# Six more chunks by seven block products in the last MLP group, their side products added at the end of each unit

## Chip, core and metric

One core of one Trainium2 chip. The metric is the device time of one execution in microseconds. The kernel before took 2679.48 us in the median of three runs (2678.41 to 2681.5).

## What is computed

Two layers of a streaming encoder on 256 rows of 2048 columns in fp32, and a final RMSNorm. The part that matters here is the MLP at the end of a layer:

```python
for l in range(DEPTH):                      # DEPTH = 2
    ...
    h = rmsnorm(x, norm_mlp[l])
    x = x + jnp.square(jax.nn.relu(h @ w_up[l])) @ w_down[l]    # 2048 -> 8192 -> 2048
return rmsnorm(x, final_norm)
```

## The kernel before

**Chunks.** All weights run through one stream of chunks. A chunk holds 256 rows of K by 512 output columns (128 partitions x 1024 fp32, 512 KB). A unit is eight chunks, K = 2048 into one block of 512 output columns. The two row tiles t of 128 rows fill two PSUM banks `acc[bank][t]`.

**Splits.** fp32 precision comes from three matmuls of rounded values: hi x hi, hi x lo, lo x hi. For each chunk SP loads `raw[c % 4]`, ACT copies it to `w_hi[c % 4]` (L865), DVE subtracts to get `w_lo[c % 4]` (L1281), and PE multiplies. There are four buffers of each. ACT waits until PE has finished chunk c-4 (`multiplied`), and SP waits for `lo_ready` of chunk c-4 before it loads chunk c. Each engine runs its own program in order, written out by hand in `unit` of ACT and of DVE: `at` puts a job ahead of a chunk's split, `then` behind it.

**Two kinds of chunk.** A plain chunk is 12 matmuls of 512 columns (L522 to L524, in the interleaved units L538 to L540, in the last unit L552 to L554). A chunk by seven products, `seven_products` at L476, sees the chunk's 256 x 512 weights and the 256 x 256 activations as 2 x 2 blocks and needs 7 block products in place of 8, a Strassen-Winograd form: 21 matmuls of 256 columns (L490 to L492). For it DVE forms sums of weight blocks (`weight_sums`, L1290 to L1296) and the split is 1792 columns wide (ACT L872 and L874, DVE L1302). Sums of activation blocks must be there too: for the hidden activations u they are made in `u_moved` (L1767 to L1772), copied by ACT (`u_sums_hi`, L1197) and split by DVE (`u_sums_lo`, L1776). Four of the seven products are accumulated in two side banks, `wide_acc`. `take_sides` (L1782) reads these into `rest` in SBUF, and `add_sides` (L1787 to L1791) combines the four quarters of a block and adds them to x.

**The MLP.** K and columns of the hidden layer are taken in four groups of 2048. The first three run in a loop `Fori` with many seven-product chunks. The last group is written out after the loop: up unit 2 (chunks 1, 3, 5, 7 by seven products), up unit 3 (plain), then four down units for the four blocks of x. Down units 0 and 1 are interleaved (PE L836 to L850) since the blocks of u arrive one by one. Then come down unit 2, and down unit 3, in the second layer as `last_unit`, which takes row tile 0 of its chunks 4 to 7 first and row tile 1 of these behind.

**Blocks of u.** After an up unit ACT applies relu and square into `stage`, DVE transposes in 32x32 pieces (`spread_u`, L1359), a DMA writes to scratch in HBM and four DMAs read it back into `moved`, ACT and DVE split that into `o_hl` (L932, L1383). Blocks 1 and 2 are passed on by POOL, block 3 by SP, in `load_down(GROUPS - 1, 0, pass_on(l, E_LAST), late=True, ...)`: SP issues all loads of down unit 0, then waits for the spread, stores, waits, fetches, and only then loads the first chunk of unit 1.

**The end of a down unit** n: DVE adds the banks to block n of x (`add_to_x`, L1700, two instructions of 128x512), ACT then squares that block for the norm (`square_block`, L949), and in the second layer DVE multiplies with the final gain (`gain_block`, L1798). These jobs lie in the chunk stream of the next unit. The four side sums of the loop, in `rest`, are added to x by `add_sides(0)` in up unit 3, `(1)` in the interleaved stretch, `(2)` and `(3)` later, wherever DVE's list has them. In the last group the DVE lines of before are:

```python
run(C_MLP + 64 * g + 32, (), {3: second_and_third, 5: lambda: add_sides(1)})
for n in range(1, NBLK):
    def x_add(n=n):
        add_to_x(base + 64 * g + (42 if n == 1 else 32 + 8 * n), n - 1)
    ...
    then = {3 if n > 1 else 5: x_add}
    ...
    if n < NBLK - 1:
        then[3 if n == 1 else 5] = lambda n=n: add_sides(n + 1)
```

`42` is the unit-0 end: the tenth chunk of the interleaved sixteen is the last of unit 0.

Of the kernel before, what the change touches and what calls it, by code (L numbers as in the profile page):

```python
# [5 lines left out]
ALU = mybir.AluOpType  # L6
ACT = mybir.ActivationFunctionType
# [8 lines left out]
DEPTH = 2  # L16
# [75 lines left out]
U_SUMS = (GROUPS - 1) * NBLK  # L92
SHARED = ((0, 1, 2, 3, 4, 5, 8, 9), (-2, -1, 2, 3, 4, 5, 6, 7))
# [17 lines left out]
def trunk_kernel(nc, x, w_misc, w_main, gains, sinks, rel_bias, onehot, final_gain, bias_rows, out):  # L111
    with ExitStack() as ctx:
# [354 lines left out]
        def _(pe):  # L467
# [248 lines left out]
            for l in range(DEPTH):  # L716
# [130 lines left out]
                for c in range(8, 10):
                    plain(two, c, c - 2, o_lhs, acc[0])
                for c in range(10, 16):
                    plain(two, c, c - 8, o_lhs, acc[1])  # L850
                down(last + 48, 0, adds(GROUPS - 1, 1), 2)
# [7 lines left out]
        def _(act):  # L859
# [186 lines left out]
            for l in range(DEPTH):  # L1046
# [168 lines left out]
                with act.Fori(0, GROUPS - 1) as g:  # L1215
# [25 lines left out]
                run(C_MLP + 64 * g + 32, (), {3: second_and_third})  # L1241
                for n in range(1, NBLK):
                    def x_take(n=n):
                        act.wait_ge(dve_took, l * DVE_UNITS + (12 + 4 * (GROUPS - 1) + n + 1))
                        square_block(n - 1, l * (2 * NBLK) + (2 * NBLK + n - 1))
# [10 lines left out]
                    run(C_MLP + 64 * g + 32 + 8 * n, (), then)  # L1256
# [17 lines left out]
        def _(dve):  # L1274
# [313 lines left out]
            for l in range(DEPTH):  # L1588
# [168 lines left out]
                def u_moved(g, n, sums=True):  # L1757
# [6 lines left out]
                    steps = g * (3 * NBLK) + (l * U_SUMS * 3 + 3 * n)  # L1764
                    a11, a21, a12, a22 = (moved_pieces()[:, a] for a in range(4, 8))
# [59 lines left out]
                with dve.Fori(0, GROUPS - 1) as g:  # L1825
# [26 lines left out]
                run(C_MLP + 64 * g + 16, (), {2: lambda: u_moved(g, 0, False), 3: lambda: spread_u(g, 1)},  # L1852
                    WIDE_UP[2], steps_at(g, AT_UP2))
                run(C_MLP + 64 * g + 24, {3: lambda: add_up_sides(g, 2, NBLK)},
                    {2: lambda: u_moved(g, 1, False), 4: lambda: spread_u(g, 2), 6: lambda: add_sides(0)})

                def second_and_third():
                    u_moved(g, 2, False)
                    spread_u(g, 3)
                run(C_MLP + 64 * g + 32, (), {3: second_and_third, 5: lambda: add_sides(1)})  # L1860
                for n in range(1, NBLK):
                    def x_add(n=n):
                        add_to_x(base + 64 * g + (42 if n == 1 else 32 + 8 * n), n - 1)
                        if l < DEPTH - 1:
                            spread_x(E_XD + n - 1, n - 1, 12 + 4 * g + n)
# [6 lines left out]
                    if n < NBLK - 1:  # L1872
                        then[3 if n == 1 else 5] = lambda n=n: add_sides(n + 1)
# [6 lines left out]
                    run(C_MLP + 64 * g + 32 + 8 * n, (), then)  # L1880
# [103 lines left out]
```

## Time and profile before

| | us |
|---|---|
| median of three runs | 2679.48 |
| profiled execution | 2679.57 |
| its span, first to last instruction | 2677.8 |
| PE busy | 2662.2 (99%) |
| PE weight load busy | 2231.3 (83%) |
| DVE busy | 2048.7 (77%) |
| ACT busy | 1446.9 (54%) |
| POOL busy | 128.4 (5%) |

Busy time is the time in which an engine's instructions run; PE's weight loads overlap its matmuls. The chain that ended last is 92% PE. A plain share of the span says nothing on a single stretch: for that the rows below are from timelines (start, duration, and in brackets how long the engine idled before an instruction and what ended it) and from windows.

### The profile page before, as it was taken

What the parts mean: (1) busy time and instruction counts of PE and PEld (TensorE: products, weight loads), DVE (VectorE), ACT (ScalarE), POOL (GpSimd) and SP (SyncE); (2) the same over time, 40 slices, a digit from 0 to 9 for tenths busy, and PEclk for the clock granted to TensorE, in tenths of its full rate; (3) what the DMA queues carried; (4) which work ended last, traced back from release to release, by engine and by line L of the source; (5) the groups of instructions that cost most, each with busy time, mean ns of one, the idle gap of its engine ahead of it and who ended that gap; (6) DMA issues with size and microseconds to landing.
All of it is one profiled execution on the core that took longest, in us unless ns stands there. A gap on an engine that the chain in (4) does not pass through costs nothing.

```text
span 2677.8 us, 37183 instructions
## 1 busy us (share of the span) xinstructions
PE 2662.2 (99%) x13544; PEld 2231.3 (83%) x13544; DVE 2048.7 (77%) x3016; ACT 1446.9 (54%) x1861; POOL 128.4 (5%) x220
## 2 busy tenths in 40 slices
PE   9999999999999999999999999999999999999998
PEld 7788778888888888888887887788888888888886
DVE  5665568977798897987756655689678988989875
ACT  5545555555665555645445455555456556556554
POOL 0100000000100100100010000000001000000000
PEclk9999999999999999999999999999999999999999
DMA  7874545676775766766687655466677667667574
GB/s 258 240 232 166 181 158 183 224 245 233 233 233 190 242 220 203 243 208 232 228 238 224 214 173 177 156 202 224 227 258 235 226 202 237 213 219 231 190 248 150
DMA packets 179959, 575.53 MB, mean 215 GB/s; under 512 B 23016, under 2 KB 43028, under 8 KB 179664
## 3 DMA queue, kind: packets, MB, share of 16 engines
q1 hardware_dynamic: 166400, 537.21, 60.8%
q0 software_dynamic: 13008, 35.98, 5.2%
q8 instruction: 106, 1.74, 0.3%
q14 instruction: 61, 0.50, 0.1%
q10 hardware_dynamic: 384, 0.11, 0.0%
HBM read 535.15 MB, written 38.04 MB: 214 GB/s over the span
## 4 chain that ended last, share of the span: by engine, by line
PE 92%; DVE 4%; DMA 2%; issue 1%; ACT 1%; DVEq 0%; POOLq 0%; ACTq 0%; POOL 0%; SPq 0%
PE acc L522 24%; PE acc L524 23%; PE acc L523 23%; PE att L490 2%; PE att L492 2%; PE att L491 2%; PE acc L490 2%; PE acc L492 2%; PE acc L491 2%; DMA raw<-in_w_main 1%; DVE w_lo L1281 1%; PE acc L539 1%; PE acc L538 1%; PE acc L540 1%; DVE w_lo L1302 1%
## 5 line engine op out<-in xcount | busy, mean ns | idle before, releaser
L1281 DVE TENSOR_TENSOR w_lo<-raw,w_hi 128x1024 fp32r<-128x1024 f32 (+1 forms) x778 | 935.3, 1213 | 422.7 <-ACT w_hi L865 419.9
L865 ACT ACTIVATE w_hi<-raw 128x1024 fp32r<-128x1024 f32 (+1 forms) x778 | 813.7, 1051 | 676.9 <-PE acc L524 499.1
L522 PE MATMUL acc<-w_hi,h_hl 128*128 128x512 f32 x1848 | 736.6, 399 | 1.0 <-DVE w_lo L1281 1.0
L524 PE MATMUL acc<-w_hi,h_hl 128*128 128x512 f32 x1848 | 729.0, 394 | 0.0
L523 PE MATMUL acc<-w_lo,h_hl 128*128 128x512 f32 x1848 | 728.5, 394 | 0.0
L522 PEld LDWEIGHTS acc<-w_hi,h_hl 128*128 128x128 f32 x1848 | 347.9, 188 | 83.7 <-issue 5.5
L524 PEld LDWEIGHTS acc<-w_hi,h_hl 128*128 128x128 f32 x1848 | 347.9, 188 | 81.4
L523 PEld LDWEIGHTS acc<-w_lo,h_hl 128*128 128x128 f32 x1848 | 348.3, 188 | 75.9
L1302 DVE TENSOR_TENSOR w_lo<-raw,w_hi 128x1792 fp32r<-128x1792 f32 x166 | 335.6, 2022 | 40.5 <-ACT w_hi L874 39.4
L522 PE MATMUL acc<-w_hi,o_hl 128*128 128x512 f32 x912 | 360.9, 396 | 0.0
L523 PE MATMUL acc<-w_lo,o_hl 128*128 128x512 f32 x912 | 359.9, 395 | 0.0
L524 PE MATMUL acc<-w_hi,o_hl 128*128 128x512 f32 x912 | 359.7, 394 | 0.0
L872 ACT ACTIVATE w_hi<-raw 128x768 fp32r<-128x768 f32 x166 | 140.3, 845 | 197.5 <-PE acc L492 112.9
L874 ACT ACTIVATE w_hi<-raw 128x1024 fp32r<-128x1024 f32 x166 | 174.8, 1053 | 82.3 <-DVE raw L1296 82.2
L524 PEld LDWEIGHTS acc<-w_hi,o_hl 128*128 128x128 f32 x912 | 171.7, 188 | 40.3
L522 PEld LDWEIGHTS acc<-w_hi,o_hl 128*128 128x128 f32 x912 | 171.6, 188 | 37.4 <-issue 1.4
L523 PEld LDWEIGHTS acc<-w_lo,o_hl 128*128 128x128 f32 x912 | 171.7, 188 | 36.0
L1290 DVE TENSOR_TENSOR raw<-raw 128x512 f32<-128x512 f32 x166 | 113.4, 683 | 15.1 <-DMA raw<-in_w_main 8.9
L1359 DVE STREAM_TRANSPOSE spread<-stage 128x512 f32<-128x512 f32 x112 | 73.0, 689 | 22.9 <-ACT stage L1068 19.8
L963 ACT ACTIVATE probs<-probs,low 128x128 f32<-128x128 f32 x96 | 41.0, 428 | 69.1 <-DVE sink_d L1510 44.0
L1294 DVE TENSOR_TENSOR raw<-raw 128x256 f32<-128x256 f32 x166 | 70.6, 425 | 5.8
L1296 DVE TENSOR_TENSOR raw<-raw 128x256 f32<-128x256 f32 x166 | 70.6, 425 | 5.7
(279 smaller groups left out, 3474.7 us busy)
## 6 DMA issues: line engine op xcount, KB each, us to landing
raw<-in_w_main SPq DMA_DIRECT2D x928, 512.0 KB, 4.2
scratch<-spread SPq DMA_DIRECT2D x37, 512.0 KB, 2.8
moved<-scratch SPq DMA_DIRECT2D x148, 128.0 KB, 3.3
scratch<-spread POOLq DMA_DIRECT2D x30, 512.0 KB, 3.5
moved<-scratch POOLq DMA_DIRECT2D x120, 128.0 KB, 4.9
raw<-in_w_misc SPq DMA_DIRECT2D x16, 336.0 KB, 3.8
bias_b<-bias_rows POOLq DMA_DIRECT2D x32, 96.0 KB, 5.3
xs<-in_x SPq DMA_DIRECT2D x4, 512.0 KB, 7.2
```

Source lines behind the costliest of these rows:

```text
L490: nc.tensor.matmul(o, a_hi, hi[:, w], start=start, stop=False, skip_group_check=True)
L491: nc.tensor.matmul(o, a_hi, lo[:, w], start=False, stop=False, skip_group_check=True)
L492: return nc.tensor.matmul(o, a_lo, hi[:, w], start=False, stop=stop, skip_group_check=True)
L522: nc.tensor.matmul(o, a_hi, hi[:, kk], start=(k == 0), stop=False)
L523: nc.tensor.matmul(o, a_hi, lo[:, kk], start=False, stop=False)
L524: last = nc.tensor.matmul(o, a_lo, hi[:, kk], start=False, stop=fin)
L865: nc.scalar.activation(w_hi[s][:, 0:2 * width], raw[r][:, 0:2 * width], ACT.Copy).then_inc(hi_ready, 1)
L872: nc.scalar.activation(w_hi[s][:, 0:3 * HALF], raw[s][:, HALF:CW], ACT.Copy)
L874: nc.scalar.activation(w_hi[s][:, 3 * HALF:7 * HALF], raw[s][:, CW:2 * CW], ACT.Copy).then_inc(hi_ready, 1)
L1281: nc.vector.tensor_tensor(w_lo[s][:, 0:2 * width], raw[r][:, 0:2 * width], w_hi[s][:, 0:2 * width].bitcast(F32), ALU.subtract).then_inc(lo ...
L1290: nc.vector.tensor_tensor(r[:, 4 * HALF:6 * HALF].rearrange("p (k n) -> p k n", k=2), r[:, HALF:3 * HALF].rearrange("p (k n) -> p k n", k= ...
L1302: nc.vector.tensor_tensor(w_lo[s][:, 0:7 * HALF], raw[s][:, HALF:8 * HALF], w_hi[s][:, 0:7 * HALF].bitcast(F32), ALU.subtract).then_inc(lo ...
```

## The change

In the second layer's last group, two of the eight chunks of K of each of down units 0, 1 and 2 are multiplied by seven block products: `END_WIDE = ((1, 3), (3, 5), (1, 3))`. In the order of loads, with the 32 down chunks numbered 0 to 31, these are 1, 3, 11, 13, 17 and 19. With it come: the sums of u for blocks 0, 1 and 2 of the last group, on DVE and ACT; weight sums and wide splits for the six chunks; a read of the side banks (`take_sides`) and the combination (`add_sides`) for blocks 0, 1 and 2 once their unit is done, just ahead of `add_to_x`. The earlier `add_sides(0)`, `(1)`, `(2)` are gone in this layer; `add_sides(3)` stays. ACT's squares of both layers' last groups write to `stage` and no longer to `att[2]`, now a side bank.

```diff
+END_WIDE = ((1, 3), (3, 5), (1, 3))
 ...
+                def chunk(at, c, n):
+                    if c in ends[n]:
+                        pe.wait_ge(sums_took, u_sums_took(GROUPS - 1, c // 2))
+                        pe.wait_ge(lo_ready, two + (RAW + at + 1))
+                        seven_products(c, acc[n], o_lhs, u_sum, wide_acc[1 - n], ends[n]).then_inc(multiplied, 1)
+                    else:
+                        plain(two, at, c, o_lhs, acc[n])
 ...
-                down(last + 48, 0, adds(GROUPS - 1, 1), 2)
+                down(last + 48, 0, adds(GROUPS - 1, 1), 2, wide=ends[2])
 ...
-                run(C_MLP + 64 * g + 32, (), {3: second_and_third})
+                run(C_MLP + 64 * g + 32, (), {3: second_and_third, 4: end_sums(2)}, ends[0], steps_at(g, END_AT[0]))
 ...
-                        square_block(n - 1, l * (2 * NBLK) + (2 * NBLK + n - 1))
+                        square_block(n - 1, l * (2 * NBLK) + (2 * NBLK + n - 1), stage)
 ...
+                    if isinstance(g, int) and n:
+                        dve.wait_ge(sums_took, g * NBLK + (l * U_SUMS + n))
 ...
+                def first_and_spread():
+                    if final:
+                        u_sums_lo(g, 1)
+                    spread_u(g, 2)
 ...
-                    {2: lambda: u_moved(g, 1, False), 4: lambda: spread_u(g, 2), 6: lambda: add_sides(0)})
+                    {2: lambda: u_moved(g, 1, final), 4: first_and_spread, 6: (lambda: None) if final else (lambda: add_sides(0))})
 ...
                     def x_add(n=n):
-                        add_to_x(base + 64 * g + (42 if n == 1 else 32 + 8 * n), n - 1)
+                        at = base + 64 * g + (42 if n == 1 else 32 + 8 * n)
+                        if final:
+                            unit_done(at)
+                            chain.link(take_sides(n - 1))
+                            add_sides(n - 1)
+                        add_to_x(at, n - 1)
 ...
-                    if n < NBLK - 1:
+                    if n == 2 or (n == 1 and not final):
                         then[3 if n == 1 else 5] = lambda n=n: add_sides(n + 1)
 ...
-                    run(C_MLP + 64 * g + 32 + 8 * n, (), then)
+                    run(C_MLP + 64 * g + 32 + 8 * n, (), then, ends[n] if n < 3 else (), steps_at(g, END_AT[n]) if n < 3 else None)
```

On DVE, the splits of down chunks 12 to 16 of the second layer, with block 0 of x between those of 13 and 14. Before:

```order
L1281 TENSOR_TENSOR w_lo0<-raw0,w_hi0 128x1024 [waits hi_ready,dve_chain]
L1281 TENSOR_TENSOR w_lo1<-raw1,w_hi1 128x1024 [waits hi_ready]
L1700 TENSOR_TENSOR xs<-acc00,xs 128x512 [waits multiplied]
L1700 TENSOR_TENSOR xs<-acc01,xs 128x512
L1281 TENSOR_TENSOR w_lo2<-raw2,w_hi2 128x1024 [waits hi_ready]
L1798 TENSOR_TENSOR xs<-xs,bias_a 128x512 [waits final_loaded,sq_done]
L1798 TENSOR_TENSOR xs<-xs,bias_a 128x512
L1281 TENSOR_TENSOR w_lo3<-raw3,w_hi3 128x1024 [waits hi_ready]
```

Now (the first row is the split of chunk 12, `w_lo1` is chunk 13, `w_lo2` is 14):

```order
L1298 TENSOR_TENSOR w_lo0<-raw0,w_hi0 128x1024 [waits hi_ready]
L1319 TENSOR_TENSOR w_lo1<-raw1,w_hi1 128x1792 [waits hi_ready]
L1801 TENSOR_TENSOR qk<-att2,qk 128x512 [waits multiplied]
L1801 TENSOR_TENSOR qk<-turn,qk 128x512
L1807 TENSOR_TENSOR qk<-qk 128x256 [waits dve_chain]
L1808 TENSOR_TENSOR qk<-qk 128x256 [waits dve_chain]
L1809 TENSOR_TENSOR qk<-qk 128x256
L1810 TENSOR_TENSOR qk<-qk 128x256 [waits dve_chain]
L1811 TENSOR_TENSOR xs<-xs,qk 128x2x512 [waits dve_chain]
L1717 TENSOR_TENSOR xs<-acc00,xs 128x512 [waits multiplied,dve_chain]
L1717 TENSOR_TENSOR xs<-acc01,xs 128x512
L1298 TENSOR_TENSOR w_lo2<-raw2,w_hi2 128x1024 [waits hi_ready]
```

The read of `att2` and `turn` and the five instructions of the combination stand between the split of chunk 13 and the addition to x; the split of chunk 14 moved behind them. Around block 1 (chunks 19, 20) and block 2 (chunks 27, 28) the same is found.

On DVE, up unit 3 from the split of its chunk 2 to that of its chunk 3. Before:

```order
L1281 TENSOR_TENSOR w_lo2<-raw2,w_hi2 128x1024 [waits hi_ready]
L1383 TENSOR_TENSOR o_hl<-moved,o_hl 128x1024 [waits moved_hi]
L1671 TENSOR_TENSOR stage2<-att2,stage 128x256 [waits sides_out]
L1673 TENSOR_TENSOR stage<-stage2,turn 128x2x256 [waits up_step]
L1676 TENSOR_TENSOR stage<-stage,turn 128x256 [waits up_step]
L1677 TENSOR_TENSOR stage<-acc00,stage 128x512
L1679 TENSOR_TENSOR stage<-acc01,stage 128x512 [waits up_step]
L1281 TENSOR_TENSOR w_lo3<-raw3,w_hi3 128x1024 [waits hi_ready]
```

Now:

```order
L1298 TENSOR_TENSOR w_lo2<-raw2,w_hi2 128x1024 [waits hi_ready]
L1400 TENSOR_TENSOR o_hl<-moved,o_hl 128x1024 [waits moved_hi]
L1786 TENSOR_TENSOR stage2<-moved 128x128 [waits sums_took]
L1787 TENSOR_TENSOR stage2<-moved 128x128
L1789 TENSOR_TENSOR stage2<-stage2,moved 128x128 [waits sum_step]
L1791 TENSOR_TENSOR stage2<-moved,stage2 128x128 [waits sum_step]
L1688 TENSOR_TENSOR stage2<-att2,stage 128x256 [waits sides_out]
L1690 TENSOR_TENSOR stage<-stage2,turn 128x2x256 [waits up_step]
L1693 TENSOR_TENSOR stage<-stage,turn 128x256 [waits up_step]
L1694 TENSOR_TENSOR stage<-acc00,stage 128x512
L1696 TENSOR_TENSOR stage<-acc01,stage 128x512 [waits up_step]
L1298 TENSOR_TENSOR w_lo3<-raw3,w_hi3 128x1024 [waits hi_ready]
```

Four sums of u block 1 stand ahead of the side additions of up unit 2 (L1671 to L1679 before, L1688 to L1696 now).

## Rows read from the trace of the kernel before

**Rows 1.** Windows: length, busy of PE, PEld, DVE, ACT, POOL; clock, DMA, GB/s.
```profile
2568.20:2646.30 78.10, 78.10 (x337) 63.30 (x337) 55.86 (x64) 36.24 (x42) 2.77 (x5) 1.00 0.70 227
```

**Rows 2.** Timeline of PE: start us, us, engine, line, operation, tiles, shape.
```profile
2453.07 0.28 PE L490 MATMUL att<-w_hi,m_hl 128*128 128x256 f32 x1
...
2455.56 0.39 PE L522 MATMUL acc<-w_hi,o_hl 128*128 128x512 f32 x1
...
2646.32 0.40 PE L552 MATMUL acc<-w_hi,o_hl 128*128 128x512 f32 x1
...
2668.41 0.40 PE L554 MATMUL acc<-w_hi,o_hl 128*128 128x512 f32 x1
```

**Rows 3.** Timeline of ACT and DVE, last unit; [idle before <-what ended it].
```profile
2646.58 1.06 ACT L865 ACTIVATE w_hi<-raw 128x1024 fp32r<-128x1024 f32 x1 [1.72 <-PE acc L524]
...
2647.68 1.23 DVE L1281 TENSOR_TENSOR w_lo<-raw,w_hi 128x1024 fp32r<-128x1024 f32 x1 [1.55 <-ACT w_hi L865]
2648.82 1.28 DVE L1700 TENSOR_TENSOR xs<-acc,xs 128x512 f32<-128x512 f32 x2
...
2650.13 0.60 ACT L949 ACTIVATE att<-xs 128x512 f32<-128x512 f32 x1 [2.49 <-DVE xs L1700]
...
2651.52 1.99 ACT L865 ACTIVATE w_hi<-raw 128x1024 fp32r<-128x1024 f32 x2
...
2652.59 2.36 DVE L1281 TENSOR_TENSOR w_lo<-raw,w_hi 128x1024 fp32r<-128x1024 f32 x2 [2.50 <-ACT w_hi L865]
```

**Rows 4.** Timeline of DVE: u sums in loop; up units 2 and 3.
```profile
2418.84 0.28 DVE L1767 TENSOR_TENSOR stage<-moved 128x128 f32<-128x128 f32 x1
...
2419.94 1.31 DVE L1359 STREAM_TRANSPOSE spread<-stage 128x512 f32<-128x512 f32 x2
...
2540.30 2.02 DVE L1302 TENSOR_TENSOR w_lo<-raw,w_hi 128x1792 fp32r<-128x1792 f32 x1 [1.95 <-ACT w_hi L874]
...
2566.71 1.23 DVE L1281 TENSOR_TENSOR w_lo<-raw,w_hi 128x1024 fp32r<-128x1024 f32 x1 [2.31 <-ACT w_hi L865]
```

**Rows 5.** Timeline of DVE, loop end: side read, wide split, weight sums.
```profile
2521.73 1.28 DVE L1782 TENSOR_TENSOR qk<-att,qk 128x512 f32<-128x512 f32 x2
...
2532.53 2.03 DVE L1302 TENSOR_TENSOR w_lo<-raw,w_hi 128x1792 fp32r<-128x1792 f32 x1 [2.30 <-ACT w_hi L874]
2534.48 0.69 DVE L1290 TENSOR_TENSOR raw<-raw 128x512 f32<-128x512 f32 x1
...
2536.00 1.22 DVE L1281 TENSOR_TENSOR w_lo<-raw,w_hi 128x1024 fp32r<-128x1024 f32 x1
```

**Rows 6.** Timeline of SP, the hand-over of u block 3.
```profile
2586.49 0.33 SPq L324 DMA_DIRECT2D scratch<-spread  x1
...
2590.88 0.91 SPq L308 DMA_DIRECT2D raw<-in_w_main  x2
```

**Rows 7.** Timeline of ACT: the split of down chunk 8.
```profile
2595.77 1.06 ACT L865 ACTIVATE w_hi<-raw 128x1024 fp32r<-128x1024 f32 x1 [3.90 <-DMA raw<-in_w_main]
```

**Rows 8.** Timeline of DVE: addition of side products, next split.
```profile
2604.20 0.42 DVE L1787 TENSOR_TENSOR qk<-qk 128x256 f32<-128x256 f32 x1
...
2607.17 1.22 DVE L1281 TENSOR_TENSOR w_lo<-raw,w_hi 128x1024 fp32r<-128x1024 f32 x1
```

**Rows 9.** Timeline of ACT: the two copies of a seven-product chunk.
```profile
2538.49 0.82 ACT L872 ACTIVATE w_hi<-raw 128x768 fp32r<-128x768 f32 x1
2539.22 1.04 ACT L874 ACTIVATE w_hi<-raw 128x1024 fp32r<-128x1024 f32 x1
```

**Rows 10.** Timeline of DVE, last unit: gain, reduction, last split.
```profile
2657.19 1.29 DVE L1798 TENSOR_TENSOR xs<-xs,bias_a 128x512 f32<-128x512 f32 x2
2658.39 0.15 DVE L1801 TENSOR_REDUCE mean_sq<-squares 128x2 f32<-128x6 f32 x1
...
2658.90 1.23 DVE L1281 TENSOR_TENSOR w_lo<-raw,w_hi 128x1024 fp32r<-128x1024 f32 x1
```

**Rows 11.** Windows, after the last matmul; columns as in Rows 1.
```profile
2674.00:2675.00 1.00, 0.00 (x0) 0.00 (x0) 0.00 (x0) 0.00 (x0) 0.00 (x0) 0.50 1.10 352
```

More of the change, by code:

```diff
@@ L835, in _ @@
                 two = l * CHUNKS + last + 32
+                ends = END_WIDE if l == DEPTH - 1 else ((), (), ())
+                def chunk(at, c, n):
[5 more added lines that the diff above has]
+                        plain(two, at, c, o_lhs, acc[n])
                 acts(GROUPS - 1, 3)()
@@ L943, in hi_moved_x, with square_block @@
                 last.then_inc(moved_hi, 1)
-            def square_block(n, before):
+            def square_block(n, before, over=None):
                 for t in range(TT):
                     act.wait_ge(sq_done, before * TT + t)
-                    nc.scalar.activation(att[2][:], xs[:, t, n * NB:(n + 1) * NB], ACT.Square,
+                    nc.scalar.activation(att[2][:] if over is None else over[:, t, :], xs[:, t, n * NB:(n + 1) * NB], ACT.Square,
                                                 accum_out=squares[:, t, n:n + 1]).then_inc(sq_done, 1)
@@ L1232, in _, with end_sums @@
                 g, end = GROUPS - 1, base + 64 * (GROUPS - 1)
-                run(C_MLP + 64 * g + 16, {3: lambda: take_up(g, 1, end + 16, 1)}, {2: lambda: u_moved(g, 0)},
+                ends = END_WIDE if l == DEPTH - 1 else ((), (), ())
+                def end_sums(n):
+                    return (lambda: u_sums_hi(g, n)) if l == DEPTH - 1 else (lambda: None)
+                run(C_MLP + 64 * g + 16, {3: lambda: take_up(g, 1, end + 16, 1)}, {2: lambda: u_moved(g, 0), 6: end_sums(0)},
                     WIDE_UP[2], steps_at(g, AT_UP2))
                 run(C_MLP + 64 * g + 24, {3: lambda: take_side(g, 2, end + 24), 4: lambda: take_summed(g, 2, sides_count(g, 0))},
-                    {2: lambda: u_moved(g, 1)})
+                    {2: lambda: u_moved(g, 1), 3: end_sums(1)})
                 def second_and_third():
@@ L1879, in _ @@
                         then[6] = lambda n=n: gain_block(n - 1)
-                    run(C_MLP + 64 * g + 32 + 8 * n, (), then)
+                    run(C_MLP + 64 * g + 32 + 8 * n, (), then, ends[n] if n < 3 else (), steps_at(g, END_AT[n]) if n < 3 else None)
                 if l < DEPTH - 1:
```

30 lines of the change are left out of this document (21 added, 9 removed).

## The prediction

> **What bounds the kernel now.** I read the busy time by stretch first. From 2568.20 to 2646.30 us, most of the last group, PE is busy for the whole stretch at a granted clock of 1.00 [rows 1]. It waits for nothing there, so the stage costs what its matmuls cost, and every chunk that PE takes faster is a gain as long as its split is ready in time. The second view is PE's timeline, for the price of a chunk. The chunk by seven products in the loop starts at 2453.07 and the next plain one at 2455.56, which is 2.49 us. The last unit runs from 2646.32 to the last matmul at 2668.41 plus one step of 0.23, 22.32 us for eight plain chunks, or 2.79 us each [rows 2]. The third view is the timeline of ACT and DVE, because they feed PE: a chunk is split by ACT, then by DVE, and ACT may start on chunk c only when PE has finished chunk c-4. So the lead is four chunks of PE time: 4 x 2.79 = 11.16 us for plain ones. In the last unit PE finishes the unit before at 2646.32, ACT starts at 2646.58, DVE at 2647.68, the addition to x at 2648.82, the squares at 2650.13, ACT's next split at 2651.52, DVE's at 2652.59 [rows 3]. That DVE split ends 1.23 later, 7.50 us after the release, so 3.7 us of the lead are left. This slack is what the change spends.
>
> I number the 32 down chunks of the group 0 to 31 as SP loads them (0 to 15 are units 0 and 1 interleaved, 16 to 23 unit 2, 24 to 31 unit 3). Seven products: 1, 3, 11, 13, 17, 19. Counting back at 2.79, PE starts chunk 0 at 2579.36 and chunk 8 at 2601.68 in the run before.
>
> **Part 1, the seven products.** Six chunks at 2.49 in place of 2.79 are 6 x 0.30 = 1.8 us less on PE, all on the path. That is the whole gain.
>
> **Part 2, sums of u and of weights.** Each of three u blocks now gets its four small sums on DVE: 1.10 us from the first of them to the next instruction in the loop (2418.84 to 2419.94) [rows 4]. A split of the sums (128x512, estimated at 0.6, half of the 1.14 for twice the width) and an ACT copy follow. Block 0's lie in up unit 2, where DVE idles 1.95 us ahead of its split of 2540.30: nothing. Block 1's stand directly ahead of the side additions and of the splits of up unit 3's chunks 3 and 4. DVE's split of chunk 4 starts at 2566.71 there and ends at 2567.94 [rows 4]; PE wants it at 2579.36 - 4 x 2.79 = 2568.20. The slack is 0.26, the addition 1.10, so PE waits 0.84; the split of the sums stands behind it, and I take **1.0**, with 0 and 1.4 as ends.
> Each seven-product chunk costs DVE the weight sums, 2534.48 to 2536.00, 1.52 us, and a split of 1.95 (2532.53 to 2534.48) in place of 1.14 [rows 5]: 2.33 more, for a chunk that PE finishes 0.3 sooner. Chunks 1 and 3 stand before block 3 is spread. SP sends that spread on before it loads chunk 8: the store is issued at 2586.49, chunk 8's load only at 2590.88 [rows 6], and ACT gets it at 2595.77 after waiting 3.90 us for the DMA [rows 7]. Ahead of the spread DVE gets two sets of sums (2.2), a split of sums (0.6) and 2 x 2.33, and loses one side addition (2.97): 4.5 us more, some of it into idle time, so the load comes 0 to 4.5 later. Block 3 is ready about 3.5 us after ACT's start, at 2599.2, and PE wants it at 2601.68, or at 2602.1 with the 1.0 and 2 x 0.3 above. Stall 0 to 1.7; I take **0.5**.
>
> **Part 3, the side products, added when a unit is done.** Before, the additions (2604.20 to 2607.17, 2.97 us) [rows 8] ran in idle time of DVE. Now they stand between the end of a unit and the addition to x, behind a read of the side banks: two instructions of 128x512 from PSUM, 1.28 us as in the loop [rows 5]. ACT stands waiting for that addition with its squares, and behind the squares is its next split. That is a wait of two engines in a chain, 4.25 us longer than before.
> Unit 2, block 2 (chunk 28, all plain), from the release: 0.26 + 1.10 + 1.14 (ACT and DVE split of chunk 27), + 1.28 + 2.97 + 1.31 (addition to x, till the squares start) + 1.39 (squares) + 1.07 + 1.23 = 11.75 us, against a lead of 11.16 [rows 3, 5, 8]. Late by 0.6.
> Blocks 0 and 1 (chunks 14 and 20) have a seven-product chunk as the last one split, so ACT takes 0.73 + 1.06 and DVE 1.95 in place of 1.10 and 1.14 [rows 5, 9], and two of the four chunks of the lead are short ones. The chain is 13.3 us against 2 x 2.79 + 2 x 2.49 = 10.56: late by 2.7 each, even if DVE arrives with nothing queued.
> DVE does arrive with work queued. Counted from the start of its split of chunk 14: PE reaches chunk 20 at 1.23 + 4 x 2.79 + 2 x 2.49 = 17.4. DVE has chunk 14 (1.14), the gain (1.20), 15, sums of 17 (1.52), 16, 17 (1.95), sums of 19, 18 and 19: 12.7 us. Then 1.28 + 2.97 + 1.31 + 1.39 + 1.07 + 1.23 = 9.25, together 21.95. Chunk 20 is late by **4.6**. For chunk 14 I take **3.3**, between 2.7 and the 4.6 of chunk 20, nearer the low end since chunks 4 to 10 are plain. For chunk 28, splits and loads of 20 to 27 come late too (a load is issued only when DVE has split the chunk four before): 0.6 to 1.5, I take **1.0**.
> Chunk 31: PE's last unit takes only row tile 0 of chunks 28 to 31 first, so it wants them every 1.40 us. DVE has 29 and 30, the gain (1.20), a reduction with its follow-up (2658.39 to 2658.90, 0.51) and then chunk 31 [rows 10]. From chunk 28's DVE start: 3 x 1.14 + 1.20 + 0.51 + 1.23 = 6.36, and PE wants it at 1.23 + 4.19 = 5.42. Late by **0.9**.
> The squares go to SBUF and not to a PSUM bank. The nearest row, a copy to SBUF, takes 1.06 us for 1024 columns, the square to PSUM 0.60 for 512 [rows 3], so 0.1 us either way for each of the two, and I take 0. In the first layer nothing else changes. The tail behind the last matmul is the same.
>
> **Sum.** -1.8 + 1.0 + 0.5 + 3.3 + 4.6 + 1.0 + 0.9 = +9.5 us. The profiled execution took 2679.57 us (span 2677.8), 0.09 above the median of the three timed runs. 2679.57 + 9.5 = **2689.1 us**, 0.36% slower.
>
> **Rivals.**
> A, the forecast: the longer chain outruns the lead and DVE's queue adds to it.
> B, only the bare chains: DVE has caught up at each of the three places and the early stalls are hidden. 2 x 2.7 + 0.6 + 0.9 - 1.8 = +5.1, 2684.7 us. For it: DVE does catch up before, as its idle 1.95 us ahead of 2540.30 shows [rows 4]. Against it: the 12.7 us of listed work between chunks 14 and 20 leave no idle time.
> C, the lead covers the additions and PE never waits: 2679.57 - 1.8 = 2677.8 us, faster than before by less than 0.2%. It decides at the chain's length: read and additions (4.25 us) would have to take under 1.5 us together, or ACT would have to split ahead of the squares, which its order does not do. For it speaks only that PE never waits there now. A partial cover ends within 0.2% of before.
> D, PE's clock falls. At the end of the program PE starts its last matmul at 2668.41 [rows 2], and the clock is 0.50, the lower level of 1.2 GHz, in the stretch from 2674 to 2675 [rows 11]: at most 5.6 us of idleness brought it. The stall ahead of chunk 20 (4.6) comes near that. At half clock one chunk costs 2.79 more; with one such chunk the time is 2691.9 us.
> The Trainium skill ("TensorE: Matmul & The Clock Gate", Part 1) says that an idle array falls back to 1.2 GHz by itself and needs sustained activity to return. By that rule D could set in at shorter stalls than the tail shows, at the price just given; the trace agrees with it as to the level only.
>
> **How the numbers follow.** A 0.64, B 0.14, D 0.14, C with partial cover 0.08. The upper end takes the high ends of the terms (1.4, 1.7, 4.6, 5.4 for chunk 20 with a late load, 1.5, 0.9): 15.5 - 1.8 = +13.7, 2693.3, and a clock drop on a middling case reaches 2695. The lower end is B's, 2684.5. Below it lies C. About 0.2% (5.4 us, so 2684.8) is what a measurement of this kernel can tell from no change: B falls on that line, and I count about two in five of it as the same, with C. More than 0.2% of gain is out of reach, since PE can save 1.8 us only. Slower 0.85, same 0.14, faster 0.01.
>
> **What would show it.** In the profile after, PE should have idle time at four places in the last 90 us, each put down to DVE's w_lo: 2.7 to 4.6 us ahead of chunk 14, 3 to 5 ahead of chunk 20, 0.6 to 1.5 ahead of 28, about 0.9 in the first pass over 31; and under 1.5 in up unit 3. The six chunks should take 2.49. ACT's wait for the addition to x, 2.5 us before, should read about 7. If PE waits nowhere, C is right and the reading of the lead is wrong. If the stalls are as said but the time is higher, look for a granted clock under 1.00.

## The result and the profile after

The changed kernel takes 2692.64 us in the median of six runs (2689.64 to 2695.77), the kernel before 2681.15 in the median of six beside them (2678.41 to 2683.51). The ratio is 1.0045, with a 95% interval of 1.0034 to 1.0055: slower by 11.5 us, where the forecast had 9.5. Against the forecast time of 2689.1 it is 3.5 us above; 1.7 of that is the kernel before, which came out slower in these six runs than in the three that the forecast started from. The profiled execution took 2691.67 us.

The measure for the rest is a stretch of PE's timeline, from the first matmul of up unit 2's sums (`s_hh`) to the last matmul of the program. Before it is 129.59 us (2538.82 to 2668.41, the end is in [rows 2]), after 140.77 us (2539.80 to 2680.57): +11.18. Of the 12.1 us between the two profiled executions the rest, 1.0, is there before the stretch starts; the tail behind the last matmul is the same within 0.1. Runs of one kernel differ by up to 6 us end to end, so the experiments below are compared by this stretch. How far the stretch itself varies between runs of one kernel was not measured; differences of a few tenths are read only where a single gap shows them.

The window over most of the last group, which answers to [rows 1]: length, busy of PE, PEld, DVE, ACT, POOL, then clock, DMA share, GB/s.

```profile
2568.00:2646.00 78.00, 71.02 (x354) 59.13 (x353) 63.53 (x79) 39.16 (x48) 2.76 (x5) 0.97 0.59 195
```

PE was busy for all of this stretch before; now it is idle for 7 us of it, and the clock is below 1.00. PE's timeline after shows where (in brackets the idle time ahead of an instruction and what ended it):

```profile
2603.05 0.50 PE L540 MATMUL acc<-w_hi,o_hl 128*128 128x512 f32 x1 [0.36 <-DVE o_hl L1400]
...
2619.16 0.28 PE L494 MATMUL acc<-w_hi,o_hl 128*128 128x256 f32 x1
2623.11 0.51 PE L540 MATMUL acc<-w_hi,o_hl 128*128 128x512 f32 x1 [3.67 <-DVE w_lo L1298]
...
2623.96 0.63 PE L540 MATMUL acc<-w_hi,o_hl 128*128 128x512 f32 x1
...
2627.33 0.39 PE L542 MATMUL acc<-w_hi,o_hl 128*128 128x512 f32 x1
2627.56 0.39 PE L540 MATMUL acc<-w_hi,o_hl 128*128 128x512 f32 x1
...
2640.77 0.28 PE L494 MATMUL acc<-w_hi,o_hl 128*128 128x256 f32 x1
2644.00 0.53 PE L524 MATMUL acc<-w_hi,o_hl 128*128 128x512 f32 x1 [2.95 <-DVE w_lo L1298]
```

These are chunks 8, 14 and 20, all at the places forecast. Behind the two long stalls a matmul of 512 columns starts 0.43 us after the one before it, and 0.23 once that is over. The waits of the last 160 us (engine, its tile and line, what it waited for, us in total, times, longest) add chunks 28 and 31 (L554) and ACT's wait for the addition to x:

```profile
ACT stage L961 <- DVE xs L1717: 22.0, 3, 7.6
...
PE acc L540 <- DVE w_lo L1298: 3.7, 1, 3.7
...
PE acc L524 <- DVE w_lo L1298: 3.0, 1, 3.0
...
PE acc L554 <- DVE w_lo L1298: 1.0, 2, 0.5
```

**The chain ahead of chunk 14**, DVE's timeline after. It answers to the last-unit rows of [rows 3]: there the addition to x followed a split directly; now the read (L1801) and the combination (L1807 to L1811) stand between them.

```profile
2611.82 2.03 DVE L1319 TENSOR_TENSOR w_lo<-raw,w_hi 128x1792 fp32r<-128x1792 f32 x1
2613.77 0.68 DVE L1801 TENSOR_TENSOR qk<-att,qk 128x512 f32<-128x512 f32 x1
2614.37 0.68 DVE L1801 TENSOR_TENSOR qk<-turn,qk 128x512 f32<-128x512 f32 x1
2615.08 0.42 DVE L1807 TENSOR_TENSOR qk<-qk 128x256 f32<-128x256 f32 x1
...
2616.79 1.22 DVE L1811 TENSOR_TENSOR xs<-xs,qk 128x1024 f32<-128x1024 f32 x1
2618.05 1.29 DVE L1717 TENSOR_TENSOR xs<-acc,xs 128x512 f32<-128x512 f32 x2
2621.83 1.23 DVE L1298 TENSOR_TENSOR w_lo<-raw,w_hi 128x1024 fp32r<-128x1024 f32 x1 [2.49 <-ACT w_hi L877]
```

And ACT's timeline in the same microseconds:

```profile
2610.73 1.06 ACT L886 ACTIVATE w_hi<-raw 128x1024 fp32r<-128x1024 f32 x1 [0.80 <-DVE raw L1313]
2619.37 0.63 ACT L961 ACTIVATE stage<-xs 128x512 f32<-128x512 f32 x1 [7.58 <-DVE xs L1717]
...
2620.76 2.93 ACT L877 ACTIVATE w_hi<-raw 128x1024 fp32r<-128x1024 f32 x3
```

Read them together: ACT has nothing to do from 2611.79 to 2619.37, because the squares are next in its order and they want the addition. The split of chunk 14 is behind the squares, so DVE waits for ACT in turn (2.49), and PE, done with chunk 13 at about 2619.3, waits for DVE.

**The clock**, windows of one microsecond; the clock is the number behind POOL's.

```profile
2622.00:2623.00 1.00, 0.00 (x0) 0.00 (x0) 1.00 (x2) 1.00 (x2) 0.00 (x0) 1.00 0.00 0
2623.00:2624.00 1.00, 0.89 (x4) 0.71 (x5) 1.00 (x3) 1.00 (x2) 0.00 (x0) 0.92 0.00 0
2624.00:2625.00 1.00, 1.00 (x4) 0.81 (x3) 1.00 (x2) 0.42 (x1) 0.00 (x0) 0.50 0.91 229
...
2627.00:2628.00 1.00, 1.00 (x5) 0.84 (x4) 1.00 (x1) 1.00 (x2) 0.00 (x0) 0.87 0.96 356
```

Here the clock is still 1.00 at the end of the idle time. It falls to 0.50, which is 1.2 GHz, when the matmuls have resumed, and comes back while they run. The same is found from 2644.3 to 2647.7. That slow matmuls last 3.4 us each time (2623.96 to 2627.33, and 2644.34 to 2647.75) makes two losses of 1.5 and 1.6 us. The fall does not need a matmul, though: behind the last matmul of the program it comes while PE is idle, as [rows 11] has it and the window after shows.

```profile
2685.00:2686.00 1.00, 0.00 (x0) 0.00 (x0) 0.10 (x1) 0.55 (x1) 0.00 (x0) 0.64 0.44 166
```

The ledger of the stretch, each term the excess of a gap between two matmul starts over its usual 0.233 or 0.119, and the late start of the second matmul behind a stall (0.1) counted with the stall:

| | us |
|---|---|
| six seven-product chunks | -1.7 |
| up unit 3 | +0.35 |
| chunk 8 | +0.6 |
| chunk 14, and the slow matmuls behind it | +3.9, +1.5 |
| chunk 20, and the slow matmuls behind it | +3.2, +1.6 |
| chunk 28 | +0.75 |
| chunk 31 | +0.8 |
| sum | +11.0 (measured 11.2) |

### The profile page after: what moved, and what is told of

Read it like the earlier page. It is cut to its first block, busy times and chain, and to the rows that moved or that the text cites. A ratio compares the mean times of both kernels' runs of the same rounds, so it can differ in the third digit from the quotient of the medians.

```text
span 2689.9 us, 37343 instructions
## 1 busy us (share of the span) xinstructions
PE 2667.3 (99%) x13598; PEld 2235.3 (83%) x13598; DVE 2069.5 (77%) x3055; ACT 1451.8 (54%) x1870; POOL 128.0 (5%) x220
## 4 chain that ended last, share of the span: by engine, by line
PE 92%; DVE 5%; DMA 2%; ACT 1%; issue 1%; SPq 0%; ACTq 0%; POOLq 0%; POOL 0%
PE acc L524 24%; PE acc L526 24%; PE acc L525 24%; PE att L492 2%; PE att L494 2%; PE att L493 2%; PE acc L492 2%; PE acc L494 2%; PE acc L493 2%; DVE w_lo L1298 1%; DMA raw<-in_w_main 1%; DVE w_lo L1319 1%; PE acc L540 1%; PE acc L541 1%; PE acc L542 1%
## 5 line engine op out<-in xcount | busy, mean ns | idle before, releaser
L1298 DVE TENSOR_TENSOR w_lo<-raw,w_hi 128x1024 fp32r<-128x1024 f32 (+1 forms) x772 | 927.2, 1212 | 405.6 <-ACT w_hi L877 403.5
L877 ACT ACTIVATE w_hi<-raw 128x1024 fp32r<-128x1024 f32 (+1 forms) x772 | 805.6, 1051 | 633.1 <-PE acc L526 473.9
L1319 DVE TENSOR_TENSOR w_lo<-raw,w_hi 128x1792 fp32r<-128x1792 f32 x172 | 347.7, 2021 | 36.8 <-ACT w_hi L886 35.9
L886 ACT ACTIVATE w_hi<-raw 128x1024 fp32r<-128x1024 f32 x172 | 181.1, 1053 | 88.1 <-DVE raw L1313 87.9
```

The costliest lines, as they stand in the source:

```text
L877: nc.scalar.activation(w_hi[s][:, 0:2 * width], raw[r][:, 0:2 * width], ACT.Copy).then_inc(hi_ready, 1)
L886: nc.scalar.activation(w_hi[s][:, 3 * HALF:7 * HALF], raw[s][:, CW:2 * CW], ACT.Copy).then_inc(hi_ready, 1)
L1298: nc.vector.tensor_tensor(w_lo[s][:, 0:2 * width], raw[r][:, 0:2 * width], w_hi[s][:, 0:2 * width].bitcast(F32), ALU.subtract).then_inc(lo ...
L1319: nc.vector.tensor_tensor(w_lo[s][:, 0:7 * HALF], raw[s][:, HALF:8 * HALF], w_hi[s][:, 0:7 * HALF].bitcast(F32), ALU.subtract).then_inc(lo ...
```

## Experiments

Each diff is against the changed kernel. "Stretch" is the one defined above, from one profiled run of each; 129.59 is before, 140.77 after.

| kernel | stretch | us of the run | stalls of PE over 0.25 us |
|---|---|---|---|
| no combination | 132.14 | 2684.01 | up unit 3 0.64; chunk 8 0.59; 14 0.73; 20 1.66 |
| additions alone | 130.02 | 2686.46 | none |
| sums and additions | 130.40 | 2684.55 | up unit 3 0.29 |
| PE filled | 139.30 | 2690.32 | (14: 3.75, 20: 4.61, mostly filled); up unit 3 0.40; 8 0.50; 28 0.70; 31 0.72 |
| squares late | 133.56 | 2685.45 | up unit 3 0.37; 14 0.85; 20 2.08, then 1.5 at half clock |
| spread | 132.33 | 2686.32 | up unit 3 0.52; 16 0.85; 21 0.77; 22 1.22 |
| unit 1 only | 132.92 | 2681.63 | up unit 3 0.64; 14 1.50; 20 0.69 |
| spread, four chunks | 133.02 | 2684.27 | up unit 3 1.46 and 0.64; 21 0.26; 22 1.20 |
| rearranged, four | 129.69 | 2679.55 | up unit 3 0.41 |
| rearranged, six | 130.32 | 2678.58 | 16 0.79; 21 0.78 |

The last column has the excess of one gap at each place. The third is one run each, but for "rearranged, four", the median of 11. The kernel before gave 2682.70 beside the first, second, fourth and fifth of these, 2684.01 beside the third, sixth, seventh and eighth.

**No combination.** Are the seven instructions ahead of the addition what makes chunks 14 and 20 late? This kernel reads the side banks but leaves the combination away, so the side products of blocks 0 to 2 are missing from x.

```diff
                         if final:
                             unit_done(at)
                             chain.link(take_sides(n - 1))
-                            add_sides(n - 1)
                         add_to_x(at, n - 1)
```

> The changed kernel without the five combining instructions of blocks 0, 1 and 2 (the side banks are still read, but their sum is not added to x: that part of the result is left out). Theory A (a chain of DVE and ACT behind the end of a unit outruns the four-chunk lead): the chain is 2.97 us shorter. PE's stall ahead of down chunk 14 falls from 3.8 to about 0.9, that ahead of chunk 20 to about 1.6, those at chunks 28 and 31 go, the clock stays at 1.00. PE's stretch from up unit 2 to the last matmul is about 1.6 us longer than in the kernel before, in place of 11. Rival L (the DVE work of the seven-product chunks alone is too much, the additions are innocent): stalls of 3 us stay at 14 and 20.

+2.55 over before in place of +11.18. DVE's timeline shows the shorter chain: the addition to x follows the read, and the split of chunk 14 still waits 2.49 for ACT.

```profile
2612.91 2.03 DVE L1319 TENSOR_TENSOR w_lo<-raw,w_hi 128x1792 fp32r<-128x1792 f32 x1
2614.85 0.68 DVE L1801 TENSOR_TENSOR qk<-att,qk 128x512 f32<-128x512 f32 x1
...
2616.16 1.29 DVE L1717 TENSOR_TENSOR xs<-acc,xs 128x512 f32<-128x512 f32 x2
2619.94 1.23 DVE L1298 TENSOR_TENSOR w_lo<-raw,w_hi 128x1024 fp32r<-128x1024 f32 x1 [2.49 <-ACT w_hi L877]
```

Chunk 14's stall fell by 3.10, the 2.97 of the combination [rows 8] within 0.13. The stalls of chunks 28 and 31 are gone, and the clock stays at 1.00. The 0.9 above what was expected (+1.6) is mostly up unit 3 (0.64) and small gaps behind each stall.

**Additions alone, and sums and additions.** What does the longer chain cost when no chunk is by seven products? The first of the two has neither sums nor side reads, the second keeps the sums of u; in both the combination of the loop's side sums stands at the end of each unit.

```diff
-END_WIDE = ((1, 3), (3, 5), (1, 3))
+END_WIDE = ((), (), ())
 ...
-                            chain.link(take_sides(n - 1))
                             add_sides(n - 1)
```

> No seven-product chunks in the last group, no sums of u there, no side banks to read, but the additions of the loop's side products stay at the end of each unit, where the change put them. Theory A: the chain is all plain, 7.50 + 2.97 = 10.5 us against a lead of 11.16, so no stall at 14, 20 and 28; at 31 the wait is 0 to 0.3. PE's stretch as in the kernel before within 0.3 us. A rival that the place of the additions alone costs the time: stalls of 3 us at 14 and 20 here too.

> No seven-product chunks in the last group and no side banks to read, but the sums of u blocks 0, 1 and 2 are made and split as in the changed kernel, and the additions stand at the end of each unit. If the sums of block 1 cause the small stalls of up unit 3, they are here too (0.3 to 0.6 in all), and PE's stretch is about 0.5 us longer than with the additions alone. If the 0.5 us ahead of chunk 8 comes from the sums, it is here too; theory A puts most of it to the weight sums and wide splits of chunks 1 and 3, so here 0.

+0.43, where at most 0.3 had been expected, and +0.81 with the sums. In the first PE waits nowhere for more than 0.25, though ACT's longest wait for the addition is 5.5 us. So the place of the additions is harmless by itself: the lead of four plain chunks takes it. The sums cost 0.38 more, 0.29 of it in one gap in up unit 3. Chunk 8 is on time in the second too, so its 0.5 in the change is not the sums' doing: it comes with the wide splits and weight sums of chunks 1 and 3. The rest of the loss needs the seven-product chunks: their wider splits, weight sums and side reads, in front of the same chain.

**Unit 1 only.** Seven products for chunks 11 and 13 alone: chunk 14's release is then as in the change, but the queue ahead of chunk 20 is not.

```diff
-END_WIDE = ((1, 3), (3, 5), (1, 3))
+END_WIDE = ((), (3, 5), ())
 ...
-                            chain.link(take_sides(n - 1))
+                            if ends[n - 1]:
+                                chain.link(take_sides(n - 1))
```

> Seven products in down unit 1 only (chunks 11 and 13), with its side read; units 0 and 2 plain, additions at the end of each unit as in the changed kernel. Here DVE has nothing queued ahead of chunk 13, so it measures the bare chain. For chunk 14 the read of side banks is missing (unit 0 has none): 13.3 - 1.3 = 12.0 us; the lead is chunks 10 to 13, 10.56. Theory A: stall of 1.4 us ahead of 14; ahead of 20 a plain chain with a side read, 11.75 against 11.16, 0.6; none of 3 us, and the clock stays at 1.00. Stretch +2.3 us. Rival (the place of the work does not matter, only its amount on DVE): next to no stall, -0.3.

Chunk 14 is late by 1.50 and chunk 20 by 0.69, as expected within 0.1. Chunk 14 has no read of the side banks here (1.28), so with it the bare chain would be late by an estimated 2.8, where the forecast had 2.7; by that about 1 us of the 3.8 in the change was queue. Chunk 20 is 3.9 better than the 4.6 it has at full clock (next). The stretch is 1.0 longer than expected: 0.64 in up unit 3 and eight small gaps of 0.1 to 0.23, 1.1 together, stand beside the two stalls.

**PE filled.** Is the clock a term of its own? PE multiplies zeros in the time in which it would wait, 14 matmuls of 512 columns ahead of chunk 14 and 16 ahead of chunk 20; nothing else changes.

```diff
+            def hold_clock(o, count):
+                for i in range(count):
+                    nc.tensor.matmul(o[:], idle_w[:], o_hl[:, 0, 0:2, :].rearrange("p k s -> p (k s)"), start=False, stop=False,
+                                     skip_group_check=True)
 ...
                 for c in range(10, 16):
+                    if c == 14 and l == DEPTH - 1:
+                        hold_clock(acc[1][0], 14)
                     chunk(c, c - 8, 1)
```

> The changed kernel with zero products (a zero tile times u, added to an open bank, so the result is the same) queued on PE ahead of the waits for chunk 14 (14 of 512 columns, 3.3 us) and chunk 20 (16, 3.7 us). They fill most of the idle time, so the granted clock should stay at 1.00. Theory A with the chain DVE-bound: the start of chunk 20 is set by DVE counted from chunk 14, so the slow stretch after chunk 14 was hidden and only the one after chunk 20 costs: 1.7 us less than the changed kernel, with filled plus idle time 3.8 ahead of 14 and 4.7 ahead of 20. Rival: both slow stretches cost in full, 3.4 us less. Rival: the clock is no cost, 0.

PE's timeline of this kernel:

```profile
2619.57 3.41 PE L537 MATMUL acc<-o_hl,idle_w 128*128 128x512 f32 x14
2623.32 0.50 PE L549 MATMUL acc<-w_hi,o_hl 128*128 128x512 f32 x1 [0.33 <-DVE w_lo L1312]
...
2639.50 0.29 PE L495 MATMUL acc<-w_hi,o_hl 128*128 128x256 f32 x1
2639.62 3.90 PE L537 MATMUL acc<-o_hl,idle_w 128*128 128x512 f32 x16
2644.23 0.50 PE L527 MATMUL acc<-w_hi,o_hl 128*128 128x512 f32 x1 [0.71 <-DVE w_lo L1312]
```

No slow matmul is left in the stretch, and it is 1.47 us shorter, where 1.7 had been expected. The gap ahead of chunk 20, from 2639.50 to 2644.23 less one step of 0.12, is 4.61, zero products included. Of the two losses, 3.1 us together, only one comes back: chunk 20's arrival is set by DVE, not by PE, so the slow matmuls behind chunk 14 had only used up a wait that PE has at full clock anyway (4.61 in place of 3.11). At full clock the change costs +9.7.

**Squares late.** ACT takes the squares of a block two chunks later, and so copies chunk 14 without waiting for the addition to x. This takes ACT out of the chain and leaves the amount of DVE's work as it is; only the gain of block 0 stands one split later on DVE, behind chunk 15's and so not ahead of chunk 14.

```diff
-                    then = {3 if n > 1 else 5: x_take}
+                    then = {(3 if n > 1 else 5) + (2 if l == DEPTH - 1 else 0): x_take}
 ...
-                        then[6] = lambda n=n: gain_block(n - 1)
+                        then[6 if n > 1 else 7] = lambda n=n: gain_block(n - 1)
```

> The changed kernel with ACT's squares of a finished block two chunks later in ACT's order (behind the splits of chunks 15, 21 and 29), and the gain of block 0 behind the split of chunk 15. DVE's work is the same. Theory A: ACT no longer stands waiting ahead of the next split, so squares and one ACT split (2.5 us) leave the chain. Stall ahead of 14 about 1.2, ahead of 20 about 2.0, none at 28 and 31, clock 1.00, PE's stretch 2.3 us longer than in the kernel before. Rival D (it is DVE's work alone, ACT's wait costs nothing): the stalls stay at 3.8 and 3 with the low clock, +11.

ACT's timeline: the copy of chunk 14 now starts at 2615.17, and the squares stand behind it. DVE's split of chunk 14 follows the addition at once (its timeline has L1298 at 2619.78 without idle time).

```profile
2615.17 1.06 ACT L877 ACTIVATE w_hi<-raw 128x1024 fp32r<-128x1024 f32 x1 [1.43 <-PE acc L494]
2619.90 0.63 ACT L961 ACTIVATE stage<-xs 128x512 f32<-128x512 f32 x1 [3.66 <-DVE xs L1717]
```

7.2 us of the 11.2 are gone with an edit that removes no work. Chunk 14's stall fell from 3.83 to 0.85 and chunk 20's from 4.61 (at full clock) to 2.08, and 28 and 31 have none. What is left is DVE's own queue. Both stalls are as long as expected, yet the stretch is 1.7 longer than expected. The windows around chunk 20 show why:

```profile
2638.00:2639.00 1.00, 0.00 (x0) 0.00 (x0) 1.00 (x2) 0.76 (x3) 0.00 (x0) 1.00 0.00 0
2639.00:2640.00 1.00, 0.64 (x2) 0.54 (x3) 1.00 (x2) 1.00 (x3) 0.00 (x0) 0.66 0.00 0
2640.00:2641.00 1.00, 1.00 (x4) 0.81 (x3) 0.97 (x3) 1.00 (x2) 0.00 (x0) 0.50 0.56 139
2641.00:2642.00 1.00, 1.00 (x4) 0.80 (x3) 0.97 (x3) 0.58 (x1) 0.00 (x0) 0.50 0.94 381
```

The clock fell here behind a gap of only 2.08 us; eight slow steps cost 1.5. It fell at about the first matmul, at 2639.36.

**Spread.** If DVE's queue is what is left, the combination need not run in one piece either: here it comes one chunk after the read and the addition to x, and the squares wait for it by a semaphore of their own.

```diff
                             chain.link(take_sides(n - 1))
-                            add_sides(n - 1)
                         add_to_x(at, n - 1)
 ...
+                    def combine(n=n):
+                        dve.wait_ge(dve_took, l * DVE_UNITS + (12 + 4 * (GROUPS - 1) + n + 1))
+                        add_sides(n - 1, whole=True)
 ...
+                        then[4 if n > 1 else 6] = combine
```

> As the late squares, and the combination of the side products cut loose from the read: behind the split of chunk 13 (19, 27) DVE only reads the side banks and adds the unit to x (2.5 us), behind the next split it combines. DVE's work is still the same. Theory A: the chain ahead of chunk 14 is 0.26 + 1.77 + 1.95 + 2.5 + 1.23 = 7.7 us against 10.56, no stall; ahead of 20 at most 0.5, since DVE's work between 14 and 20 (12.7 + 2.5 + 3.0 + 1.2) fills the lead; PE's stretch from up unit 2 to the last matmul is within 1 us of the kernel before. Rival W (DVE's amount of work alone counts): a stall of about 2 us ahead of 20 as with the late squares, +2 us or more.

A miss: +2.7, where at most 0.5 of stall at chunk 20 and a stretch within 1 us had been expected. None is left at chunks 14 and 20, but three new ones stand at 16, 21 and 22. DVE's timeline ahead of 21 and 22:

```profile
2640.48 1.23 DVE L1814 TENSOR_TENSOR xs<-xs,qk 128x1024 f32<-128x1024 f32 x1
2641.62 1.22 DVE L1301 TENSOR_TENSOR w_lo<-raw,w_hi 128x1024 fp32r<-128x1024 f32 x1
2642.76 0.42 DVE L1810 TENSOR_TENSOR qk<-qk 128x256 f32<-128x256 f32 x1
...
2644.47 1.23 DVE L1814 TENSOR_TENSOR xs<-xs,qk 128x1024 f32<-128x1024 f32 x1
2645.73 1.23 DVE L1301 TENSOR_TENSOR w_lo<-raw,w_hi 128x1024 fp32r<-128x1024 f32 x1
```

The split of chunk 22 (2645.73) stands behind a second combination, that of block 3's sums from the loop, directly behind that of block 1. DVE runs without a gap there, so a job moved away from one chunk makes another one late: the rival that had +2 us or more was nearer, though not in the place of the stall.

**Spread, four chunks.** The same with chunks 1 and 3 plain again.

```diff
-END_WIDE = ((1, 3), (3, 5), (1, 3))
+END_WIDE = ((), (3, 5), (1, 3))
```

> The spread order with four seven-product chunks only (11, 13, 17, 19), none in unit 0. PE saves 1.2 us. Theory A: no stall ahead of chunks 8, 14 and 28, at most 0.3 ahead of 20, the small ones of up unit 3 (0.4) stay: PE's stretch 0.3 to 0.9 us shorter than in the kernel before. Rival W (DVE's work): 1 us or more of stall ahead of 20, stretch longer than before.

Also a miss, +3.4. Chunk 16 is on time now, 22 is late by 1.20 as before (the second combination is untouched), and 2.1 us are lost in up unit 3. There ACT's timeline shows the copies of the unit's chunks 1 and 2 waiting for their loads:

```profile
2556.33 1.06 ACT L878 ACTIVATE w_hi<-raw 128x1024 fp32r<-128x1024 f32 x1 [3.26 <-DMA raw<-in_w_main]
2559.97 1.06 ACT L878 ACTIVATE w_hi<-raw 128x1024 fp32r<-128x1024 f32 x1 [2.58 <-DMA raw<-in_w_main]
```

Counted from the start of the stretch chunk 2's copy comes 1.5 us later than before (19.82 in place of 18.28), and the sums of u block 1 follow on DVE soon behind its split. Why the load was later here was not tested.

**Rearranged.** Both findings put to use: the sums of u block 1 behind the split of up unit 3's chunk 3, and block 3's combination in the interleaved stretch, where DVE has idle time. Once with four chunks, timed, once with six.

```diff
-                    {2: lambda: u_moved(g, 1, final), 4: first_and_spread, ...
+                    {2: lambda: u_moved(g, 1, False), 3: (lambda: u_sums(g, 1)) if final else (lambda: None), 4: first_and_spread, ...
 ...
                         u_sums_lo(g, 2)
+                        add_sides(3)
 ...
-                    if n == 2 or (n == 1 and not final):
+                    if n < NBLK - 1 and not final:
                         then[3 if n == 1 else 5] = lambda n=n: add_sides(n + 1)
```

> The spread order with four seven-product chunks (11, 13, 17, 19), and two more moves: the sums of u block 1 stand behind the split of up unit 3's chunk 3 (behind the side additions, not ahead of them), and the combination of block 3 stands in the interleaved stretch behind chunk 5, where the kernel before had one, and not behind chunk 21. Theory A: every place then fits the lead, and PE's stretch from up unit 2 to the last matmul is 0.8 to 1.2 us shorter than in the kernel before; in the time that is 0.03 to 0.05%, which cannot be told from no change. Rival W (the amount of DVE work, not its place): 1 us or more of stall stays between chunks 16 and 24, stretch longer than before.

> The same order with all six seven-product chunks. If place alone counts, PE's stretch is 1.8 us shorter than in the kernel before. If DVE's work fills the lead with six of them (12.7 us of splits, sums and gain between chunks 14 and 20, and 5.5 of side products and x, of 17.4), there is 1 to 2 us of stall between chunks 8 and 24, and the stretch is within 1 us of before.

With four chunks the kernel takes 2679.55 us (11 runs, 2678.69 to 2682.28) against 2679.69 for the kernel before (15 runs): ratio 0.9998, 0.9989 to 1.0007. The window that answers to [rows 1] is full again:

```profile
2568.20:2646.30 78.10, 78.10 (x376) 64.69 (x377) 65.26 (x79) 40.76 (x48) 2.76 (x5) 1.00 0.66 222
```

No down chunk is late, and the stretch is 129.69 us, where -0.8 to -1.2 had been expected against 129.59. Four seven-product chunks save 1.2; a gap of 0.41 in up unit 3, four small ones of 0.1 to 0.24 and about 0.3 spread over the rest take it back. With six the stretch is 130.32, +0.7, and chunks 16 and 21 are late by 0.8 each, as the second of the two expectations had it. The one run of it, 2678.58, tells nothing against 2679.69.

## Why the prediction came out as it did

The forecast was +9.5 us; the stretch gave +11.2, and +9.7 with the clock kept full. The sign, the mechanism and the places hold; the difference is rival D's term, which occurred and which the sum had left out. That the rest agrees within 0.2 is partly luck: chunk 14 was put 0.5 too low and up unit 3 and chunk 28 too high by about as much.

- **Seven products, -1.8.** Right: 21 steps of 0.119 in place of 12 of 0.233, -1.7 for six.
- **Up unit 3, 1.0.** Too large in this run. DVE's sums took 0.93 (2560.93 to 2561.86), not 1.10, and PE lost 0.35. The slack of 0.26 was right: PE started chunk 4 at 2568.24 before, where the forecast had 2568.20. What it had not in it is the landing of a load. ACT's copy of chunk 2, at the head of this chain, waits for the DMA before and after:

```profile
2557.10 1.06 ACT L865 ACTIVATE w_hi<-raw 128x1024 fp32r<-128x1024 f32 x1 [0.81 <-DMA raw<-in_w_main]
...
2557.56 1.06 ACT L877 ACTIVATE w_hi<-raw 128x1024 fp32r<-128x1024 f32 x1 [1.82 <-DMA raw<-in_w_main]
```

  From the start of the stretch that is 18.28 us before and 17.76 after, half a microsecond sooner. Over the kernels with the sums ahead of the side additions the main gap here follows this time: 0.14 at 17.76 (the change), 0.29 at 17.88 (sums and additions), 0.52 at 18.11 (spread), 0.64 at 18.36 (no combination), 2.1 in two gaps at 19.82 (spread, four chunks). With the load as late as before the gap would be about 0.6, by these rows; that it was 0.14 is luck.
- **Chunk 8, 0.5.** 0.53 in the gap, 0.6 with the follow-up. The path to it was as said: SP's timeline after, to be read beside [rows 6],

```profile
2589.86 0.33 SPq L326 DMA_DIRECT2D scratch<-spread  x1
...
2594.24 2.13 SPq L310 DMA_DIRECT2D raw<-in_w_main  x4
```

  has the load issued 3.4 us later, and ACT gets it at 2599.54 in place of 2595.77 [rows 7]; 1.0 of both is there before the stretch starts, so 2.4 and 2.8 are the change's, within the 0 to 4.5 given.
- **Chunk 14, 3.3.** Measured 3.8. It was chosen between the bare chain's 2.7 and 4.6, and the unit-1 kernel lets the two parts be estimated: about 1 us of queue, the rest chain.
- **Chunk 20, 4.6.** Measured 3.1 after slow matmuls, 4.6 with PE kept at full clock. DVE needed 20.9 us from the split of chunk 14 (2621.83) to that of chunk 20 (2642.72); the sum of rows had 21.95 - 1.23 = 20.7.
- **Chunk 28, 1.0, and chunk 31, 0.9.** 0.75 and 0.8. From the start of chunk 28's split to the end of chunk 31's DVE took 6.24 (forecast 6.36). DVE's timeline, to be read beside [rows 10]:

```profile
2667.41 3.50 DVE L1298 TENSOR_TENSOR w_lo<-raw,w_hi 128x1024 fp32r<-128x1024 f32 x3 [2.50 <-ACT w_hi L877]
2670.82 1.29 DVE L1818 TENSOR_TENSOR xs<-xs,bias_a 128x512 f32<-128x512 f32 x2
2672.03 0.15 DVE L1821 TENSOR_REDUCE mean_sq<-squares 128x2 f32<-128x6 f32 x1
...
2672.42 1.23 DVE L1298 TENSOR_TENSOR w_lo<-raw,w_hi 128x1024 fp32r<-128x1024 f32 x1
```

- **Rival D, the clock.** Here is the step that failed: its price was not in the forecast's sum, because the tail's 5.6 us of idleness [rows 11] was read as the size at which the clock falls. That row is an upper bound only. The clock fell behind gaps of 3.8 and 3.1 us, and of 2.1 in the kernel with the late squares. Its net price in the change was 1.5 us, by the filled kernel. The price given for D, one chunk at half clock or 2.79, was an overestimate: each slow stretch lost 1.5 or 1.6, and one of the two was hidden. That the median of 2692.6 is close to D's 2691.9 is luck: D's price was 1.3 too high, and the kernel before came out 1.7 higher beside it. The Trainium skill's rule that an idle array falls back by itself and needs sustained activity to return ("TensorE: Matmul & The Clock Gate", Part 1) had pointed this way, and both halves agree with the trace after: 0.50 behind the last matmul and behind both long stalls, 1.00 again while matmuls run.
- **Rival B, bare chains**, is refused by chunk 20 (4.6 in place of 2.7). **Rival C**, the lead covers it, holds only where all chunks are plain: with the additions alone no gap is over 0.25. The forecast's reading of the lead thus needs both parts, a longer chain and short chunks with wide splits in the lead.

ACT's wait for the addition to x was forecast at about 7; it is 7.58 at block 0. That the same chain can be broken by ACT's order alone, for 7.2 us, was named in rival C as the point that decides.

What stays open: how much the stretch varies from run to run, small gaps of 0.2 or so near the end of several kernels, what moves the loads in up unit 3, and when a gap of about 2 us costs the clock.

## What to carry to other kernels

Cost a change in a prefetched stream by the chain from the release of a buffer to its refill, engine by engine, and compare it with the lead in time: shorter chunks shrink the lead while their extra preparation lengthens the chain. If one engine waits in order for another's result, ask first whether its next independent job can stand ahead of that wait; here that was worth four times what the faster chunks could save. And where a forecast has stalls of 2 us or more on PE (2.1 was enough here), put a clock loss into the range at least, and ask whether the next stall hides it.

## What the runs showed of the hardware

- In the three stalls that cost the clock, it was still 1.00 when the idle time ended, and fell to 0.50 at the first matmul behind it or up to 0.8 us after; behind the last matmul of the program it fell while PE was idle (0.64 in 2685 to 2686 after). The gaps ahead were 3.8, 3.1 and 2.1 us; one of 1.66 us ahead of the same chunk (no combination) and one of 1.50 (unit 1 only) brought no slow matmul. Matmuls of 512 columns then took 0.43 us a step in place of 0.23, for 3.4 to 3.5 us each time, a loss of 1.5 to 1.6, the 0.1 of the last point below not counted.
- Matmuls on zeros, 14 and 16 of them in the time of the two long stalls, kept the clock at 1.00 (PE filled).
- At full clock the first matmul behind a stall takes 0.50 to 0.53 us in place of 0.40, and the second starts 0.34 after it and not 0.23, so each stall costs about 0.1 us beyond its own length.
